# Summing two squared tiles on VectorE before the ones product, and projecting the last mixer's queries for 512 tokens

## The reference, cut to what matters

```
def _head_rms_norm(x, g):
    y = x * lax.rsqrt(jnp.mean(x * x, axis=-1, keepdims=True) + EPS)
    return y * g.astype(jnp.float32)[None, :, None, :]
```

```
q_l = axial_rope(q_l.reshape(B, T, GLA_HEADS, GLA_DK)) * GLA_DK ** -0.5
pc = hc @ jnp.concatenate([w_in[:, O_K:O_G], w_in[:, O_A:]], axis=1)
```

## Time and profile before

| | |
|---|---|
| runs | 3528.71, 3529.36, 3531.3 us; median 3529.36 |
| profiled execution | span 3528.9 us, the time from its first to its last instruction; no other time of that execution is listed |
| instructions | 41233 |
| TensorE (PE) matmul busy | 3285.4 us, 93% of the span |
| weight load (PEld) | 2683.2 us, 76% |
| VectorE (DVE) | 1397.9 us, 40% |
| ScalarE (ACT) | 1219.1 us, 35% |
| HBM | 93 GB/s over the span |

### The profile page before, as it was taken

How to read it: one execution, slowest core, us unless ns; L and a number is a source line. 1 busy time by engine, 2 the same in 40 slices (tenths; PEclk the granted TensorE clock), 3 DMA queues, 4 the chain that set the end, 5 groups by cost and what they waited for, 6 DMA issues and landing times. The chain is left out here.

```text
span 3528.9 us, 41233 instructions
## 1 busy us (share of the span) xinstructions
PE 3285.4 (93%) x17560; PEld 2683.2 (76%) x17560; DVE 1397.9 (40%) x1969; ACT 1219.1 (35%) x1849; POOL 1.2 (0%) x6
## 2 busy tenths in 40 slices
PE   6986999999999899999998987899999989889998
PEld 5764787888877688788887865788887877578876
DVE  2753344443342634434423355521125334442233
ACT  3414454222235445422225235521113243342222
POOL 0000000000000000000000000000000000000000
PEclk9998999999999999999999999999999989999999
DMA  3211223765232022387522400322224222033322
GB/s 119 72 67 48 84 96 94 205 179 144 84 111 71 25 84 96 86 208 186 150 87 66 102 13 1 120 62 70 60 60 155 95 63 97 1 107 96 96 96 78
DMA packets 416822, 329.55 MB, mean 93 GB/s; under 512 B 23416, under 2 KB 357816, under 8 KB 416384
## 3 DMA queue, kind: packets, MB, share of 16 engines
q1 hardware_dynamic: 400640, 317.74, 30.3%
q10 hardware_dynamic: 16000, 9.18, 1.1%
HBM read 324.74 MB, written 2.15 MB: 93 GB/s over the span
## 5 line engine op out<-in xcount | busy, mean ns | idle before, releaser
L285 DVE TENSOR_TENSOR w_lo<-raw,w_hi 128x1024 fp32r<-128x1024 f32 (+1 forms) x494 | 570.3, 1196 | 947.9 <-ACT w_hi L273 947.6
L273 ACT CAST w_hi<-raw 128x1024 fp32r<-128x1024 f32 (+1 forms) x494 | 483.6, 1029 | 791.8 <-PE ps L328 611.9
L326 PE MATMUL ps<-hT_hi,w_hi 128*128 128x512 f32 (+2 forms) x1616 | 574.3, 355 | 10.7 <-DVE hT_lo L693 7.5
L327 PE MATMUL ps<-hT_lo,w_hi 128*128 128x512 f32 (+2 forms) x1616 | 566.7, 351 | 0.0
L328 PE MATMUL ps<-hT_hi,w_lo 128*128 128x512 f32 (+2 forms) x1616 | 566.1, 350 | 0.0
L326 PE MATMUL ps<-xT_hi,w_hi 128*128 128x512 f32 x1024 | 418.5, 409 | 45.2 <-DVE arena L742 27.3
L328 PE MATMUL ps<-xT_hi,w_lo 128*128 128x512 f32 x1024 | 402.3, 393 | 0.0
L327 PE MATMUL ps<-xT_lo,w_hi 128*128 128x512 f32 x1024 | 402.0, 393 | 0.0
L326 PE MATMUL ps<-w_hi,hT_hi 128*128 128x512 f32 x904 | 363.4, 402 | 28.4 <-DVE hT_lo L1194 13.9
L327 PE MATMUL ps<-w_lo,hT_hi 128*128 128x512 f32 x904 | 356.2, 394 | 0.0
L328 PE MATMUL ps<-w_hi,hT_lo 128*128 128x512 f32 x904 | 356.0, 394 | 0.0
(11 more groups left out here) (336 smaller groups left out, 3588.6 us busy)
## 6 DMA issues: line engine op xcount, KB each, us to landing
scratch_sb<-in_ada_w SPq DMA_DIRECT2D x96, 512.0 KB, 6.6
raw<-in_ffn_w_in SPq DMA_DIRECT2D x88, 512.0 KB, 7.3
raw<-in_ffn_w_down SPq DMA_DIRECT2D x30, 1024.0 KB, 5.0
raw<-in_ffn_w_gate SPq DMA_DIRECT2D x44, 512.0 KB, 4.0
raw<-in_ffn_w_up SPq DMA_DIRECT2D x44, 512.0 KB, 5.3
raw<-in_ffn_w_out SPq DMA_DIRECT2D x20, 1024.0 KB, 5.1
raw<-in_ev_w_in SPq DMA_DIRECT2D x16, 1024.0 KB, 5.3
raw<-in_xa_w_kv SPq DMA_DIRECT2D x16, 1024.0 KB, 5.2
```

Source lines behind the costliest of these rows:

```text
L273: act.copy(self.split_chunk(c)[0][:, half], self.raw_chunk(c)[:, half]).then_inc(self.split_hi, 1)
L285: ins = dve.tensor_tensor(lo[:, half], self.raw_chunk(c)[:, half], hi[:, half].bitcast(F32), ALU.subtract)
L326: pe.matmul(out, w[0], x[0], start=first, stop=False)
L327: pe.matmul(out, w[0], x[1], start=False, stop=False)
```

## The change

Two edits. In `head_norm`, heads of two tiles get one more VectorE instruction each, which adds the two squared tiles in place, and one product with ones instead of two; TensorE waits for that sum (`dve:pair`) instead of the squares. The additions are written ahead of the gain products of their group of four heads, and without `pace` each stands behind the lane's share of its head. In the last mixer the stage `cdqk` becomes two: `cdq`, the query chunk over 512 tokens, and `cdk`, the key chunk over all 768. The loads of constants go with `cdq`.

```
@@ weight_plan
-            mix(I["cd_w_in_2"][0], [("cd_qk", 512, 1024, 0), ("cd_a", 2048, 2080, 0), ("cd_g", 1536, 2048, 0),
+            mix(I["cd_w_in_2"][0], [("cd_q", 512, 768, 0), ("cd_k", 768, 1024, 0), ("cd_a", 2048, 2080, 0), ("cd_g", 1536, 2048, 0),
@@ head_norm
-    s_mean, s_centered, s_sq, s_sums, s_rr, s_dve_chain, s_gated, s_done = stage_sems(
-        k, name, "pe:mean", "dve:centered", "act:sq", "pe:sums", "act:rr", "dve:dve_chain", "act:gated", "dve:done")
+    s_mean, s_centered, s_sq, s_pair, s_sums, s_rr, s_dve_chain, s_gated, s_done = stage_sems(
+        k, name, "pe:mean", "dve:centered", "act:sq", "dve:pair", "pe:sums", "act:rr", "dve:dve_chain", "act:gated", "dve:done")
@@ head_norm, tensor
-            pe.wait_ge(*s_sq((h + 1) * per))
-            for i in range(per):
-                ins = pe.matmul(bank(h), k.ones[:], sqt(h, i), start=i == 0, stop=i == per - 1)
-            ins.then_inc(*s_sums.up(1))
+            pe.wait_ge(*(s_pair(h + 1) if per == 2 else s_sq(h + 1)))
+            pe.matmul(bank(h), k.ones[:], sqt(h, 0), start=True, stop=True).then_inc(*s_sums.up(1))
@@ head_norm, vector
             if h % 4 == 0:
+                if per == 2:
+                    for x in range(h, h + 4):
+                        if not pace:
+                            k.share("dve", (x + 1) / nh)
+                        dve.wait_ge(*s_sq(2 * x + 2))
+                        dve.tensor_tensor(sqt(x, 0), sqt(x, 0), sqt(x, 1), ALU.add).then_inc(*s_pair.up(1))
                 k.share("dve", pace["dve"][h // 4] if pace else (h + 4) / nh)
@@ cd_mixer
-    mod_norm(k, "cd_norm", list(range(TALL)), 1, 0, W["cd_qk"])
+    mod_norm(k, "cd_norm", list(range(TALL)), 1, 0, W["cd_q"])
...
-    project_feature(k, "cdqk", W["cd_qk"], 512, lambda m, a, b: qk[:, m, a:b], (0, ALL),
-                    scale=lambda m: 0.125 if m < 2 else 1.0,
+    project_feature(k, "cdq", W["cd_q"], 256, lambda m, a, b: qk[:, m, a:b], (0, SEQ), scale=lambda m: 0.125,
                     loads=[(decw[0:32], k.ins["decw"]), (rope, k.ins["axrope"]),
                            (k.arena[:, at - 4 * SEQ - ALL - 2 * P:at - 4 * SEQ - P], k.ins["gla_now"]),
                            (later, k.ins["gla_later"])])
+    project_feature(k, "cdk", W["cd_k"], 256, lambda m, a, b: qk[:, 2 + m, a:b], (0, ALL))
```

## The result

The kernel after takes 3524.14 us (median of 17 runs, 3521.89 to 3531.9), the kernel before on the same chips 3531.26 (17 runs, 3527.26 to 3535.71). The ratio is 0.9982, 95% interval [0.9976, 0.9989]: 6.4 us less, between 3.9 and 8.5. 3524.14 lies inside the wide range, 3521 to 3534, and 0.14 us inside the forecast's own, 3524 to 3532; the forecast itself, 1.55 us less, lies outside the interval. The profiled execution took 3523.57 us, 1.8 us more than its span.

A forecast was written before the change was run, and what follows sets the result against it. TensorE, busy 93%, was taken to bound the last mixer, VectorE's list the memory attentions. Mixer -5.75 plus attentions +4.2 made -1.55 on the span 3528.9, plus 0.46: 3527.8 us, range 3521 to 3534.

The forecast's parts named there:

- Part 1: Last mixer's queries: 48 products of 256 columns fewer on a gapless TensorE, worth -5.75 us, bounds -5.75 and 0.
- Part 2a: Queries' head sums, each memory attention: -3.44 us saved, waits of 0.3 and 1.0 for additions, -2.16 in all.
- Part 2b: Keys' sums, each memory attention: additions wait behind the queries' gains, TensorE resumes 2.1 us later; +4.2 for both attentions.
- The clock behind the resumption: Slow products after TensorE resumes in the memory attentions: same number as before, 0 net, bounds -1.4 and +2 us.
- All removed products pay: Rival: mixer saves 5.75 us and each memory attention 5.15, giving 3513.3 us; chance 0.08.
- The series: Rival: keys' additions, sums and squares run one after another, +7.5 us per attention, giving 3538.6 us; chance 0.07.
- The mixer's saving lost: Rival: a load or VectorE chain behind the last mixer cancels its saving, giving 3533.6 us; chance 0.08.
- The attentions even: Rival: the keys' chain is hidden better, memory attentions neither gain nor lose, giving 3523.6 us; chance 0.10.
- The edit without effect: Rival: the head-norm edit does nothing to the sums, no two-tile call reached, giving 3523.6 us; chance 0.02.

The follow-up runs named there:

- mixer_only: Kernel before with only the last mixer's edit, head norms left as they were: 3522.71 us against 3530.26, ratio 0.9975.
- mixer_queries_early: Kernel after, but the queries' additions one quarter of the lane earlier and the keys' sums with two products as before: 3513.89 us, repeated 3514.05; before 3530.26.
- pair_only: Kernel before with only the head norms' edit, queries and keys, mixer left as it was: 3533.59 us against 3530.26, ratio 1.0008.
- shift_14: Kernel before with 14 extra, overwritten 512-wide products between the two attentions, ahead of the odd mixer: 3533.38 us against 3529.98, ratio 1.0007.
- keys_between_gains: Kernel before with the head norms' edit, the keys' additions placed ahead of and between the queries' gains; mixer unchanged: 3534.83 us against 3529.98, ratio 1.0015.
- before again: The kernel before run once more with nothing edited: 3530.38 us against 3530.26, ratio 1.0002.
- after_again: The kernel after run once more with nothing edited, for a second profile: 3524.52 us against the kernel before's 3529.98, ratio 0.9985.
- shift_6: Kernel before with 6 extra, overwritten 512-wide products between the two attentions, ahead of the odd mixer: 3530.62 us against 3529.98, ratio 1.0005.
- pair_keys: Kernel before with paired sums for the keys' norms alone, queries and mixer unchanged: 3545.54 us against 3530.05, ratio 1.0038.
- pair_queries: Kernel before with paired sums for the queries' norms alone, keys and mixer unchanged: 3526.09 us against 3530.05, ratio 0.9987.
- split_before_squares: mixer_queries_early with the next weight chunk cast before the keys' squares and split after the first query head's gains: 3510.63 us; kernel before 3530.25, ratio 0.9946.

## Why the prediction was right, and what it left out

The verdict (no change of 0.2%) and the range held, and so did the mechanism in the edited stages; the total was missed by 4.8 us (-1.55 forecast, -6.4 measured), more than the interval allows. The absolute figure, 3527.8 against 3524.14, is off by less only because 17 runs put the kernel before at 3531.26 and not at 3529.36. The 0.46 us that the forecast added to the span mixed two executions; the profiled one here has 1.8 (3523.57 against 3521.8).

- **Part 1, the mixer.** Forecast -5.75, stretch -5.75 in the kernel after, in its repeat within 0.01, and in `mixer_only`; -5.37 in the two profiles of `mixer_queries_early`, an amount by which the two profiles of before differ as well (0.4). No wait for bank 0, no queue in the way. Right.
- **Part 2a, the queries' sums.** By head: forecast -0.86, -0.56, +0.14, -0.86; stretches -0.86, -0.44, +0.28, -0.86, with waits of 0, 0.19, 0.90 and 0 where 0, 0.3, 1.0 and 0 were forecast. Sum -1.9 for -2.16 (the prediction's own terms, -3.44 + 0.3 + 1.0, give -2.14). Right to 0.3 us. The bound with no wait, -3.44, was reached when the additions moved up.
- **Part 2b, the keys.** Forecast and found, the timeline of after moved by 0.21 to the origin of before: gains end 484.47, found 484.76; first sum about 485.0, found 485.42; squares of head 2 at 486.8, found 486.73; cast 487.7, found 488.21; resumption 491.2, found 491.69, against 489.14 before. TensorE resumes 2.55 us later, forecast 2.1. One step is different in kind: the squares of the last two heads ran as one block of 1.57 us and the last two sums together (487.84), but it cost nothing more. The clock during the sums was at the lower level, as taken: 2.04 us for four starts of 256 columns.
- **The clock behind the resumption.** Forecast 0 net, bounds -1.4 and +2. In the first attention 8 slow products instead of 14: -1.2, so that its end is +1.4 only; in the second the window is at 0.50 as before (0.52), no change, and the end is +2.7. Together +4.1, forecast +4.2. That it is so close is in part luck: against the second profile of before, with its 6 slow products, the first attention costs 2.9 and the two together 5.5. The scatter of slow products that the prediction quoted from the Trainium skill ("TensorE: Matmul & The Clock Gate", Part 1) is told there of a kernel's start; behind the first resumption here the two profiles of before agree with it: 14 in the one, 6 in the other, 1.5 us between them. The counts that the prediction set beside it, 13 and 7, were of two places in one profile and could not show it. But within one kernel the numbers also came out the same: 8 in both profiles of after and in `pair_only`.
- **The term that was not there.** The sum took the clock into account at one place, behind the resumption, and everything else as moved with its length kept ("Behind the stage all work is released by TensorE or by what ran after it, and moves up as a whole"). The odd mixer did not keep its length: -4.1 us, as large as the whole cost of the attentions. -5.75 + 4.1 - 4.1 = -5.75, which the interval [-8.5, -3.9] holds. This is the step of the prediction that failed: a bound was missing for stretches that change nothing but the time at which they are reached.

What is shown of it: the gain goes with the granted clock of the stretch (last column); it repeats over two profiles of the same kernel to 0.04 us; it appears without the edit (`shift_14`) and stays away with paired sums (`keys_between_gains`). What stays open is the rule. Against the change of arrival at the odd mixer (the sum of the changes from 441 to 976), the stretch went as follows; the clock is the mean over each kernel's own 976 to 1324, 0.97 in the first profile of before:

| kernel | arrival | odd mixer | granted clock |
|---|---|---|---|
| before again | -1.6 | +0.5 | 0.98 |
| mixer_only | 0.0 | -0.1 | 0.97 |
| keys_between_gains | +0.1 | -0.1 | 0.97 |
| after, after_again, pair_only | +1.4 | -4.1, -4.1, -4.15 | 0.99 |
| shift_6 | +1.4 | -1.4 | 0.98 |
| shift_14 | +4.7 | -3.9 | 0.99 |
| pair_keys | +4.0 | -0.95 | 0.98 |
| mixer_queries_early, twice | -2.0 | -4.2, -4.0 | 0.99 |
| pair_queries | -3.1 | -0.6 | 0.98 |
| split_before_squares | -6.5 | -0.4 | 0.98 |

At 0.97 the stretch is as long as before, at 0.99 it is 3.9 to 4.2 us shorter, at 0.98 it lies between -1.4 and +0.5. The arrival does not order it like that: `shift_6` arrives as late as the kernel after and gets a third of the gain, `pair_keys` and `shift_14` arrive nearly alike and differ by 3 us. So something of how the work before runs, other than its length, has a part in it, and an effect of the changed head norms by that way is not excluded. Nor was it settled why the profile of `mixer_only` is 7.7 us shorter while its own stretch is 5.75; 1.4 of it lies about the weight load that landed late in before's profile (7.98 us of waiting; 6.57 in `before_again`, 6.52 in `mixer_only`), which no edit touches.

**The rivals.** All removed products pay: out, TensorE stood 5.96 us behind the gains, as VectorE's list said. The series: out, the squares of heads 2 and 3 and their sums ran as pairs, and the resumption came 2.55 us later, not 7.5. The mixer's saving lost: out. The attentions even: out, +4.1. The edit without effect: out. The measured time, 3524.14 on a before of 3531.26, looks like the "even" rival's -5.75, and for the wrong reason: the attentions did cost 4.1, and a third place gave it back.

## What to carry to other kernels

An instruction taken off the busiest engine and put on an idle one is worth what the idle engine's list lets it be worth: the same kind of addition saved 0.86 us per head where it was done in time, 0.44 and then lost 0.28 where a weight split stood before it, and cost 4 and 6 us per attention where eight gains did (`pair_keys`). So price the place in the list before the instruction, and when it is bad, move it or leave the instruction out. Moving the queries' additions up and keeping two products for the keys turned -6 us into -17, and the cast and split ahead of the squares made it -19; in the first of these, some 7 us of the gain came from untouched stretches.

Compare two profiles stretch by stretch over the same instructions, the untouched ones too. A change of 0.2% can be as much the clock of code that was only reached at another time as the edit; a local improvement that doesn't reach the total (`keys_between_gains`) may have been paid back there.

## What the hardware did that was not expected

TensorE's granted clock in a stretch of unchanged instructions depends on how the work before it is timed, in a repeatable way: 976 to 1324 us took 347.9 us before and 343.8 after, with the granted clock of the whole at 0.97 and 0.99. One more stretch, 3005 to 3061, did the like, and in step with its clock: 0.94 before and in `before_again` (0.0), 1.00 in both profiles of `mixer_queries_early` (-3.3 us), 0.91 in `shift_6` and `keys_between_gains` (+1.6), 0.88 in `pair_keys` (+3.2).

TensorE's stand of 5.96 us ahead of the keys' sums, nearly twice the 3.13 of before, did not bring more slow products behind the resumption: 8, between the 14 and the 6 that two profiles of before showed behind the shorter stand. But the sums ran at the lower of the two levels too, which they did not before, so over the first attention the granted clock is lower: 0.89 after, 0.95 and 0.97 in the two profiles of before.
